# The modulation's sums over partitions: 32 x 32 turns and a reduction on DVE with one PE product, and another spacing of the chunks

## The reference, cut to what matters

```
mod_x = (jax.nn.silu(c) @ w_ada[l] + b_ada[l])[:, None, :]
mod_c = jax.nn.silu(c_ctx) @ w_ada[l] + b_ada[l]
sh1, sc1, g1, shm, scm, gm, sh2, sc2, g2 = jnp.split(mod_x, N_MOD, axis=-1)
csh1, csc1, cg1, cshm, cscm, cgm, csh2, csc2, cg2 = jnp.split(mod_c, N_MOD, axis=-1)

h = h + 0.5 * g1 * _swiglu(_modulate(_rms_norm(h, norm_ffn1[l]), sh1, sc1),
                           w_ffn1_gate[l], w_ffn1_up[l], w_ffn1_down[l])
...
u = _modulate(_rms_norm(h, norm_mix[l]), shm, scm)
...
p = u @ w_in[l]
...
return (jax.nn.silu(u @ w_gate) * (u @ w_up)) @ w_down
```

## Time and profile before

| | |
|---|---|
| median of 3 runs | 2193.87 us (2191.09 to 2196.12) |
| the profiled execution, its own time | 2189.74 us |
| its span, first to last instruction | 2188.0 us |
| PE busy | 2114.1 us, 97% of the span |
| DVE busy | 1343.8 us, 61% |
| ACT busy | 777.4 us, 36% |
| POOL busy | 416.3 us, 19% |
| mean granted clock of TensorE | 0.982 of full speed |
| 144 loads of the modulation's weights | 512 KB each, 4.0 us from issue to landing |

### The profile page before, as it was taken

One profiled execution on the slowest core, in us unless ns is written; L12 is line 12 of the kernel. 1 busy time (PEld: TensorE's weight loads), 2 busy tenths in 40 slices (PEclk: granted clock), 3 DMA queues, 4 the chain that ended last, 5 costly groups with the idle time before them and its releaser, 6 DMA issues.

```text
span 2188.0 us, 29282 instructions
## 1 busy us (share of the span) xinstructions
PE 2114.1 (97%) x11971; PEld 1806.2 (83%) x11971; DVE 1343.8 (61%) x1767; ACT 777.4 (36%) x1089; POOL 416.3 (19%) x197
## 2 busy tenths in 40 slices
PE   7988999999999999999999999999999998999998
PEld 6976877888888898668988888888888887679998
DVE  6658788587772267775777762366564236765444
ACT  4343467422222232553322222232222223444443
POOL 0010000222221101351222211122221111243432
PEclk9998999999999999999999999999999999999999
DMA  5328788466653345103566543346663335205654
GB/s 167 97 81 275 229 279 281 116 182 173 184 155 93 99 141 152 58 1 97 149 178 183 172 134 94 92 139 189 192 185 100 99 98 159 76 6 152 190 165 145
DMA packets 415035, 314.93 MB, mean 144 GB/s; under 512 B 27551, under 2 KB 373542, under 8 KB 414902
## 3 DMA queue, kind: packets, MB, share of 16 engines
q1 hardware_dynamic: 375344, 237.43, 37.3%
q10 hardware_dynamic: 39558, 75.64, 10.8%
...
## 4 chain that ended last, share of the span: by engine, by line
PE 87%; DVE 7%; ACT 3%; DMA 2%; issue 1%; SPq 1%; DVEq 0%; ACTq 0%
PE ps L2094 23%; PE ps L2096 23%; PE ps L2095 23%; PE ps L2276 2%; PE ps L2087 2%; DVE w_lo L1228 2%; ACT w_hi L732 2%; PE ps L2641 1%; PE ps L2642 1%; PE ps L2643 1%; PE ps L2904 1%; DVE st L1942 1%; DMA raw<-in_w_in 1%; PE ps L2866 1%; PE ps L2673 1%
## 5 line engine op out<-in xcount | busy, mean ns | idle before, releaser
L2094 PE MATMUL ps<-u_hi,w_hi 128*128 128x512 f32 (+2 forms) x2112 | 742.3, 351 | 17.1 <-DVE u_lo L1319 7.6
L2096 PE MATMUL ps<-u_hi,w_lo 128*128 128x512 f32 (+2 forms) x2112 | 731.0, 346 | 0.0
L2095 PE MATMUL ps<-u_lo,w_hi 128*128 128x512 f32 (+2 forms) x2112 | 730.9, 346 | 0.0
L1228 DVE TENSOR_TENSOR w_lo<-raw,w_hi 128x2048 fp32r<-128x2048 f32 (+1 forms) x215 | 451.6, 2100 | 290.5 <-ACT w_hi L732 290.4
L732 ACT CAST w_hi<-raw 128x2048 fp32r<-128x2048 f32 (+1 forms) x215 | 374.8, 1744 | 454.6 <-PE ps L2096 392.0
L2094 PEld LDWEIGHTS ps<-u_hi,w_hi 128*128 128x128 f32 x2112 | 403.1, 191 | 69.2 <-DVE w_lo L1228 8.1
L2096 PEld LDWEIGHTS ps<-u_hi,w_lo 128*128 128x128 f32 x2112 | 402.9, 191 | 48.6
L2095 PEld LDWEIGHTS ps<-u_lo,w_hi 128*128 128x128 f32 x2112 | 403.3, 191 | 46.7
L2024 POOL TENSOR_TENSOR hf_lo<-tmp_b,hf_hi 128x512 fp32r<-128x512 f32 (+1 forms) x88 | 240.4, 2732 | 689.8 <-ACT hf_hi L874 689.8
L1247 DVE SCALAR_TENSOR_TENSOR ada_acc<-ada_w,sc_c,ada_acc 128x512 f32<-128x512 f32 x420 | 319.7, 818 | 7.1 <-DMA ada_w<-in_w_ada 1.3
L2094 PE MATMUL ps<-hf_hi,w_hi 128*128 128x512 f32 (+1 forms) x770 | 268.2, 348 | 0.1
...
## 6 DMA issues: line engine op xcount, KB each, us to landing
ada_w<-in_w_ada ACTq DMA_DIRECT2D x144, 512.0 KB, 4.0
...
```

The source lines that it names most:

```text
L1228: tt(low, full, high.bitcast(F32), ALU.subtract).then_inc(lo_done.sem, 1)
L2094: mm(acc, w1, m_hi, start=(first and i == 0), stop=False)
L2095: mm(acc, w1, m_lo, start=False, stop=False)
L2096: ins = mm(acc, w2, m_hi, start=False, stop=(last and i == n - 1))
```

## The change

Three things change.

First, the sum over partitions is split. When DVE has done the last quarter of a chunk, it turns `ada_acc` in blocks of 32 x 32 into the slot 1 of `ada_w` (`ada_fold`: one pass over 128 x 1024, or 128 x 512 for one row), and sums over the 32 neighbours in each block (one reduction to 128 x 32 or 128 x 16, `ada_red`). After that each partition holds a sum over a quarter of the partitions. PE then makes one product per chunk, with the constant `fold` as weights and `ada_red` as moving operand, which adds the four partition quarters. `ada_out` takes the result in four passes of 32 partitions. PE's sum waits for `ada_folded`, which the reduction signals; the load of quarter 1 waits for it too, since it fills the slot that the turn has used. `fold` is made once, at the start. `ada_acc` serves for all chunks.

Second, `ada_at` spreads the quarters by a ratio: in the up stages 8 quarters to 5 units, and 2 quarters to 3 units in the down stages. The chunk is named complete at the unit at whose start all four quarters lie in earlier loops, which can be the loop just before.

Third, two chunks of ten go from `f1a` and `f2a` to the down stages `f1b` and `f2b`, and one of nine from `l1_f1a` to `l1_f1b`.

```diff
@@ -514,13 +518,10 @@
             return tmp_a[:, k % 4 // 2, SEQ * (k % 2):SEQ * (k % 2) + width]
 
         IN1 = (0, 2, 3, 4, 5, 1, 6, 7)
-        ADA = {"f1a": (4, 10, 1, 2, 1), "f2a": (17, 10, 1, 2, 1), "l1_f1a": (27, 9, 1, 2, 2)}
+        ADA = {"f1a": (4, 8, 8, 5, 1), "f1b": (12, 2, 2, 3, 0), "f2a": (17, 8, 8, 5, 1), "f2b": (25, 2, 2, 3, 0),
+               "l1_f1a": (27, 8, 8, 5, 2), "l1_f1b": (35, 1, 2, 3, 0)}
 
         ADA_LINEAR = {"q": (14, 2, 2), "out": (16, 1, 2), None: (0, 0, 1)}
-
-        def ada_acc_of(j):
-
-            return tmp_a if j in (1, 3) else ada_acc
 
         def ada_rows(j):
 
...
@@ -541,14 +542,15 @@
             if ada == "moe":
                 q0, q1 = (1, 4) if n == 0 else (3 * n + 1, 3 * n + 4) if n < 4 else (n + 9, n + 10) if n < 7 else (0, 0)
                 return [(q // 4, q % 4) for q in range(q0, q1)], {1: 0, 3: 1, 4: 2, 8: 3}.get(n)
-            first, chunks, every, each, start = ADA[ada]
-            n -= start
-            if n < 0:
-                return [], None
-            q0 = (n // every) * each
-            work = [(first + q // 4, q % 4) for q in range(q0, q0 + each) if q < 4 * chunks] if n % every == 0 else []
-            c, rest = divmod((n - 1) * each, 4 * every)
-            return work, first + c - 1 if rest == 0 and 1 <= c <= chunks else None
+            first, chunks, quarters, units, start = ADA[ada]
+
+            def until(n):
+
+                return min(4 * chunks, max(n - start, 0) * quarters // units)
+
+            work = [(first + q // 4, q % 4) for q in range(until(n), until(n + 1))]
+            done = until(n) // 4
+            return work, first + done - 1 if done > until(n - 1) // 4 else None
 
         def ada_tail(ada, n):
 
...
@@ -741,7 +743,10 @@
                     l = j // ADA_CHUNKS
                 slot = quarter % 2
                 q = 4 * j + quarter
-                need(act, ada_mac, 4 * (q - 1))
+                if quarter == 1:
+                    need(act, ada_folded, j)
+                else:
+                    need(act, ada_mac, 4 * (q - 1))
                 k = 2 * quarter
                 wv = a["w_ada_2"][l].rearrange("(k p) n -> p k n", p=P)
                 c = bass.ds((j - ADA_CHUNKS * l) * ADA_COLS, ADA_COLS)
...
@@ -1234,27 +1239,43 @@
             def ada_quarter(j, quarter):
                 slot = quarter % 2
                 dve.wait_ge(ada_full[slot], 32 * j + 16 * (quarter // 2) + 16)
-                rows, acc = ada_rows(j), ada_acc_of(j)
+                rows, acc = ada_rows(j), ada_acc
                 for kk in range(2):
                     k = 2 * quarter + kk
                     for v in rows:
                         if k == 0:
                             if v == 0:
-                                need(dve, ada_sum, j - 1 if 1 <= j <= 3 else j)
+                                need(dve, ada_turned, j)
                             ins = ts(acc[:, v, :], ada_w[:, slot, kk, :], sc_c[:, k, v:v + 1], None, ALU.mult)
                         else:
                             dve.wait_ge(ada_mac.sem, 16 * j + 2 * k + (v - 1 if len(rows) == 2 else 0))
                             ins = stt(out=acc[:, v, :], in0=ada_w[:, slot, kk, :], scalar=sc_c[:, k, v:v + 1],
                                       in1=acc[:, v, :], op0=ALU.mult, op1=ALU.add)
                         ins.then_inc(ada_mac.sem, 2 // len(rows))
+                if quarter == 3:
+                    ada_fold(j)
+
+            def ada_fold(j):
+
+                r = len(ada_rows(j))
+                turned_acc = ada_w[:, 1, :, :].rearrange("p k n -> p (k n)")[:, 0:r * ADA_COLS]
+                dve.wait_ge(ada_mac.sem, 16 * j + 16)
+                nc.vector.transpose(turned_acc, ada_acc[:, 0:r, :].rearrange("p v n -> p (v n)")).then_inc(ada_turned.sem, 1)
+                dve.wait_ge(ada_turned.sem, j + 1)
+                need(dve, ada_sum, j)
+                nc.vector.reduce_sum(ada_red[:, 0:16 * r], turned_acc.rearrange("p (b i) -> p b i", i=32), AX_X
+                                     ).then_inc(ada_folded.sem, 1)
 
             def ada_out(j):
                 dve.wait_ge(ada_sum.sem, j + 1)
                 nj = ADA_COLS // P
                 v = bass.ds(nj * j, nj)
                 r = len(ada_rows(j))
-                tt(mod[:, v, 0:r], ps[:, 4, 0:2 * nj].rearrange("p (t v) -> p t v", v=2)[:, :, 0:r], b_ada[:, v, 0:r],
-                   ALU.add).then_inc(mod_done.sem, 1)
+                for b in range(4):
+                    q = slice(32 * b, 32 * b + 32)
+                    sums = ps[q, 4, 0:16 * r].rearrange("p (v t b) -> p t v b", v=r, b=4)[:, :, :, b]
+                    ins = tt(mod[q, v, 0:r], sums, b_ada[q, v, 0:r], ALU.add)
+                ins.then_inc(mod_done.sem, 1)
 
             def norm(nm, h, T, first=0, split=True):
                 n = norm_of[nm]
...
@@ -1474,6 +1495,8 @@
             ins.then_inc(rows_out.sem, 2)
             dve.wait_ge(rows_out.sem, rows_out.at(8))
             fin = VEC["final"][0]
+            nc.vector.reduce_sum(fold[:, :].rearrange("p (c j) -> p c j", j=32),
+                                 ident.rearrange("p (o a j) -> p o j a", o=1, j=32).to_broadcast([P, 4, 32, 4]), AX_X)
             tt(eps_sq[:, :], eps, eps, ALU.mult)
             tt(fin_eps[:, :], vec[:, fin:fin + KD], vec[:, fin:fin + KD], ALU.mult).then_inc(ev["fin_sq"], 1)
             split_lo(0)
...
@@ -1885,7 +1908,7 @@
                 ffn_up(L["f1a"], L["sig"][0], T2, FFN_F, "l1_f1a" if last else "f1a",
                        before_third=None if last else close_first_block)
                 gates(l, 0, 0.5)
-                ffn_down(L["f1b"], add_gated(T2), None, keep=2)
+                ffn_down(L["f1b"], add_gated(T2), "l1_f1b" if last else "f1b", keep=2)
                 halves_norm(f"l{l}b", l, 3, "mix", L["f1b"], add_half_down(L["f1b"], f"l{l}b"), next_two(L["f1b"]),
                             second=not last)
                 gates(l, 3, 1.0)
...
@@ -2269,12 +2292,11 @@
 
             def ada_sums(j):
 
-                pe.wait_ge(ada_mac.sem, 16 * j + 16)
+                pe.wait_ge(ada_folded.sem, j + 1)
                 need(pe, mod_done, j)
-                for t in range(ADA_COLS // P):
-                    for v in ada_rows(j):
-                        ins = mm(ps[:, 4, 2 * t + v:2 * t + v + 1], ada_acc_of(j)[:, v, P * t:P * t + P], one, start=True, stop=True)
-                ins.then_inc(ada_sum.sem, 1)
+                r = len(ada_rows(j))
+                mm(ps[:, 4, 0:16 * r], fold[:, :], ada_red[:, 0:16 * r],
+                   start=True, stop=True).then_inc(ada_sum.sem, 1)
 
             def ffn_up(stg, T, n_units, ada, opening=None, halves=2, whole=False, n0=0, before_third=None):
 
```

More of the change, by code:

```diff
@@ L177, in program @@
         sc_c = sb("sc_c", [P, KD, 2])
+        fold = sb("fold", [P, P])
+        ada_red = sb("ada_red", [P, 32])
         coef = sb("coef", [P, KD, 2])
@@ L340, in program @@
         ada_mac = signal("ada_mac", 0)
+        ada_turned = signal("ada_turned", 0)
+        ada_folded = signal("ada_folded", 0)
         ada_sum = signal("ada_sum", 0)
@@ L1997, in _ @@
                 gates(l, 6, 0.5)
-                ffn_down(L["f2b"], add_gated(TQ), None, keep=0 if last else 2)
+                ffn_down(L["f2b"], add_gated(TQ), None if last else "f2b", keep=0 if last else 2)
             n = norm_of["end2"]
@@ L2950, in _ @@
                        whole=last)
-                ffn_down(L["f2b"], L["sig"][1], TQ, 11, hf_hi, hf_lo, FFN_F, None,
+                ffn_down(L["f2b"], L["sig"][1], TQ, 11, hf_hi, hf_lo, FFN_F, None if last else "f2b",
                          "end2" if last else "l1a", TQ, turn_out if last else None, keep=0 if last else 2)
```

6 lines of the change are left out of this document (3 added, 3 removed).

## The result

The changed kernel takes **2436.69 us** (median of 4 runs, 2435.36 to 2438.26), the kernel before in the same comparison 2192.48 (2190.86 to 2196.12): a ratio of 1.1112, 95% interval 1.1092 to 1.1131. The forecast was 2443 us. The profiled execution took 2438.26 us, its span is 2436.5.

The account below looks back on a forecast made before the run. PE, busy 97% of the span, was taken to set the time. 2189.7 + 158.4 + 63.3 + 55 - 37.9 + 4.4 + 2.6 + 1.3 + 2 = 2438.8 us, 2443 against the runs' median; range 2380 to 2500.

Parts of the forecast that it names:

- The place: Up units: a chunk's fold ends DVE's loop n-1, while PE wants it twelve products into unit n, so PE waits.
- The waits: Up stages, PE: 8.6 or 11.2 us per two-row chunk, 158.4 us in all; 63.3 us in `l1_f1a`.
- The fold: DVE, per two-row chunk: turn 1.21 us, reduction 1.22, with handovers 2.7 in all; 1.7 with one row.
- The clock: PE behind the 24 waits: work at half clock loses 2.3 us each, 55 us; bounds nothing and 4 each.
- The gain: PE's shorter sums: 1.50 us gained per two-row chunk, 0.61 per one-row chunk, 37.9 us in all.
- Down units: Down stages: DVE's fold delays its split for PE by 1.1 us for each of four two-row chunks, 4.4 us.
- q and out: Folds of chunks 14 and 16 ahead of DVE's splits: 2.6 and 1.3 us later, plus 2 us for the clock.
- The experts: Experts' stage: four folds of 2.7 us against four PE gains of 1.5, partly in DVE's gaps: 0, between -6 and +8.
- B: Rival: waits, but the clock stays up or the fold runs at double pace; 2388 or 2359 us; chance 0.09.
- C: Rival: dearer fold (5.1 us) or longer half-clock stretch (4 us each); 2484 to 2533 us with both; chance 0.11.
- D: Rival: the sum finds its fold ready, so only the gain is left; 2166 us; chance 0.04.
- S+2.72: Up unit: when PE's next sum would come, twelve products after the unit's start S; DVE's split runs until S+4.92.

Follow-up runs that it names:

- experiment 1: The changed kernel with each up-stage chunk's sum and output one unit later, the very last unit's chunk excepted: 2190.33 us, ratio 0.9982 to the kernel before.
- Experiment 4: The changed kernel with useless products filling PE's waits ahead of sums in the up units, tail excepted: 2389.62 us, ratio 1.0887 to the kernel before.
- experiment 8: The changed kernel, chunks complete one unit later, stage-end sums in following down stages, experts' old sums, fold behind conversion in down units and q: 2163.60 us, ratio 0.9868.

## Why the prediction was right

**The place.** The claim was that PE's sum in unit n meets a fold that ends DVE's loop of unit n-1. The waits stand in 24 places of the up stages, alternating as forecast, and experiment 1 moves nothing but this place and gets it all back. Shown.

**The waits.** Forecast 221.7 us in 24; measured 212.2. One after the other: 8.28 for 8.6, 11.08 or 11.09 for 11.2; 6.08 and 7.83 with one row for 6.4 and 8.2; 9.33 for the tail's 10.9. The chunks 11 and 24, which end a stage, waited 9.87 and 9.88 and not 11.2. A wait costs 0.16 us more than its idle time, since products start 0.227 us apart and are 0.39 long: 3.9 us for 24, which the forecast did not need, as it counted from 624.67, where the sum would have started. A wait follows from where each engine stands in one unit of the trace of before.

**The fold.** Turn 1.25 us against 1.21, reduction 1.22 against 1.22, and 0.71 and 0.69 us with one row. The estimate that was set against it, from the Trainium skill's 311 ns for a smaller turn (VectorE: DVE Perf Modes, The three transpose paths), would have made the turn 2.49 us: the measurement decides for the plain pass. Another page fits: the Trainium skill says that a turn sustains one element per cycle and lane (Vector Engine (DVE) Microarchitecture Reference, The reshape front-end and per-opcode configuration); here it takes 2% more than a reduction of the same 1024 columns.

**The clock.** Forecast 55 us. The stretches at 0.50 behind the 24 waits come to 38.6 us in `f1a`, 38.4 in `f2a` and 34.1 in `l1_f1a`, 111 us. A product takes 0.427 us there for 0.227, so 47% of that is lost: 52 us. Experiment 4 gives 47 back, without the tail's. The bound of nothing is excluded. The single stretches are 3.2 to 6.3 us long and do not follow the wait: behind 11.08 and 11.09 us they are 6.3, 4.1 and 3.5 us. The reason that was given for 2.3 us each, that the new waits are longer than the idle time in the earlier trace rows, is therefore not borne out; that the mean of the 24, 2.2 us, came so near is in part luck.

**The gain.** Forecast 1.50 and 0.61 us a chunk, 37.9 in all. It can only be seen where nothing waits, in the experiments 1 and 8: a sum costs 0.24 us there in place of 1.84 or 0.95, so 1.60 and 0.71, 40.9 in all. In `l1_f1a` one sum of 1.84 and eight of 0.95 us became seven of 0.24, 7.8 us less by the rows, and 7.8 were measured. Behind the waits of the changed kernel a sum costs 0.45 us, since the clock is down there; that is counted in the 52 us above.

**Down units.** Four waits of 1.09 or 1.10 us were measured for the 1.1 forecast. **q and out**: here the brackets mislead (2.49 + 1.79 us at q, where 0.26 stood before), since the sum itself has become shorter. From the start of the last product ahead of the sum to the first behind it there are 2.56 us at q before (818.14 to 820.70) and 5.08 now (906.48 to 911.56), 2.5 more for the 2.6 forecast; at out 1.93 (1019.72 to 1021.65) and 3.35 (1110.57 to 1113.92), 1.4 more for 1.3. Behind q PE works 3.4 us at 0.50, 1.6 us lost, behind out none, for a forecast of 2. These terms were right.

**The experts.** Forecast 0, between -6 and +8. The first silu is 5.3 us later in the profiled execution, but 2.5 of that comes from ahead of the experts, and behind there the kernels with this stage lie between -0.2 and +2.9 us. The bounds hold. The cover by DVE's gaps was smaller than thought: the wait for `ht_lo` grew from 9.4 to 17.1 us, and the four shorter sums, 6.4 us by the rows, pay most of that back. With the turn doubled the first silu comes 6.9 us later for 5.0 of turns, 4.9 of them idle time.

**The sum** with what was measured: 2189.7 + 212.2 + 3.9 + 52 - 40.9 + 4.4 + 2.5 + 1.6 + 1.4 + 5.3 = 2432.1, against 2438.3 in that execution. The 6 us left are not taken apart. The sum of 2438.8 for this execution was closer than its terms, and that is luck: the waits were 5.6 us too high (9.5 against the idle time alone), the clock 3 too high and the gain 3 too small, and against that stand the 5.3 us up to the first silu and the 6 us that are not placed.

**The rivals.** B and C are settled by the rows of the turn and of the clock. D, the fold in time, was priced at 2166 us and needed the sum later than S+2.72; made so by experiment 8, it came to 2163.6. That is no test of the price: it holds 10.3 us for down stages, q and out, most of which experiment 8 also takes away, and it sets the experts at 0, where that experiment goes back to the old sums.
